# Grouped-query contexts computed already turned, from values held stationary and probabilities in high and low parts

## The reference, cut to what matters

```python
def gqa_attention(q, k, v):                 # q: 8 heads of 128, k and v: 2 heads of 128, 256 tokens
    ...
    def block(qblk):
        sc = jnp.einsum('bqkgd,bskd->bkgqs', qblk, k).astype(jnp.float32) * scale
        pr = jax.nn.softmax(sc, axis=-1).astype(v.dtype)
        return jnp.einsum('bkgqs,bskd->bqkgd', pr, v)
    ...
branch_b = gqa_attention(q, k, v) @ w_o_attn          # no causal mask here
mixed = jax.nn.sigmoid(gate_a) * branch_a + jax.nn.sigmoid(gate_b) * branch_b
```

## Time and profile before

| | |
|---|---|
| median of 3 runs | 1844.18 us (1843.59 to 1845.41) |
| the profiled execution | 1844.49 us, span 1842.7 us |
| TensorE matmul, busy | 1823.8 us, 99% of the span |
| VectorE, busy | 1186.5 us, 64% |
| ScalarE, busy | 983.3 us, 53% |
| GpSimd, busy | 127.6 us, 7% |
| DMA engines, mean busy share | 171 GB/s moved, 54.6% of 16 engines on the queue that loads weights |
| granted TensorE clock, mean | 0.999 of full speed |

### The profile page before, as it was taken

One profiled execution on the slowest core, in us unless ns is written; L12 is line 12 of the kernel. 1 busy time (PEld: TensorE's weight loads), 2 busy tenths in 40 slices (PEclk: granted clock), 3 DMA queues, 4 the chain that ended last, 5 costly groups with the idle time before them and its releaser, 6 DMA issues.

```text
span 1842.7 us, 24850 instructions
## 1 busy us (share of the span) xinstructions
PE 1823.8 (99%) x9042; PEld 1510.8 (82%) x9042; DVE 1186.5 (64%) x2022; ACT 983.3 (53%) x1571; POOL 127.6 (7%) x52
## 2 busy tenths in 40 slices
PE   8999999999999999999999999999999999999998
PEld 7887888888887888888878888888877788888886
DVE  6766873556766874455767667555677685675556
ACT  5546554444655654444645656544557366564444
POOL 0000018300000008500000000000000000000000
PEclk9999999999999999999999999999999999999999
DMA  7554665556555655556644445656556354556563
GB/s 243 157 139 137 194 194 173 186 190 197 167 143 142 195 173 182 171 183 185 219 126 143 143 149 172 204 161 209 173 173 195 109 163 132 166 173 187 177 210 111
DMA packets 167772, 315.33 MB, mean 171 GB/s; under 512 B 10250, under 2 KB 22748, under 8 KB 167524
## 3 DMA queue, kind: packets, MB, share of 16 engines
q1 hardware_dynamic: 167332, 313.14, 54.6%
q10 hardware_dynamic: 320, 0.60, 0.1%
HBM read 312.65 MB, written 1.05 MB: 170 GB/s over the span
## 4 chain that ended last, share of the span: by engine, by line
PE 98%; DVE 1%; DMA 0%; issue 0%; ACT 0%; ACTq 0%; DVEq 0%
PE acc L579 86%; PE mix L546 4%; PE mix L880 1%; PE mix L868 1%; PE mix L831 1%; PE mix L638 1%; PE mix L626 1%; PE mix L844 1%; PE mix L606 1%; PE mix L806 0%; PE mix L820 0%; PE mix L897 0%; PE mix L840 0%; PE mix L811 0%; PE mix L662 0%; PE mix L652 0%
## 5 line engine op out<-in xcount | busy, mean ns | idle before, releaser
L1081 ACT ACTIVATE hi<-raw 128x1024 fp32r<-128x1024 f32 (+2 forms) x600 | 616.6, 1032 | 523.0 <-PE acc L579 496.0
L1524 DVE TENSOR_TENSOR lo<-raw,hi 128x1024 fp32r<-128x1024 f32 (+3 forms) x552 | 647.3, 1188 | 243.3 <-ACT hi L1081 228.0
L579 PE MATMUL acc<-hi,xTh 128*128 128x512 f32 (+3 forms) x1760 | 690.1, 392 | 4.6 <-DVE lo L1524 1.4
L579 PE MATMUL acc<-hi,xTl 128*128 128x512 f32 (+3 forms) x1760 | 674.2, 383 | 0.0
L579 PE MATMUL acc<-lo,xTh 128*128 128x512 f32 (+3 forms) x1760 | 673.2, 382 | 0.0
L579 PEld LDWEIGHTS acc<-hi,xTh 128*128 128x128 f32 x1760 | 332.1, 189 | 75.9 <-issue 14.5
L579 PEld LDWEIGHTS acc<-hi,xTl 128*128 128x128 f32 x1760 | 331.7, 188 | 64.3
L579 PEld LDWEIGHTS acc<-lo,xTh 128*128 128x128 f32 x1760 | 332.4, 189 | 59.0 <-issue 1.0
L1052 POOL TENSOR_TENSOR lo<-raw,hi 128x1024 fp32r<-128x1024 f32 x48 | 127.4, 2681 | 635.7 <-ACT hi L1081 635.6
L579 PE MATMUL acc<-hi,hTh 128*128 128x512 f32 x432 | 169.2, 392 | 0.0
L579 PE MATMUL acc<-hi,hTl 128*128 128x512 f32 x432 | 168.4, 390 | 0.0
(11 more groups left out here) (232 smaller groups left out, 1516.7 us busy)
## 6 DMA issues: line engine op xcount, KB each, us to landing
raw<-in_w_in SPq DMA_DIRECT2D x192, 512.0 KB, 3.8
raw<-in_w_ffn_in SPq DMA_DIRECT2D x80, 512.0 KB, 4.4
raw<-in_w_mlp_up SPq DMA_DIRECT2D x64, 512.0 KB, 3.8
raw<-in_w_mlp_down SPq DMA_DIRECT2D x64, 512.0 KB, 4.5
raw<-in_w_ffn_out SPq DMA_DIRECT2D x44, 512.0 KB, 4.4
raw<-in_w_out SPq DMA_DIRECT2D x32, 512.0 KB, 4.1
raw<-in_w_o_gla SPq DMA_DIRECT2D x16, 512.0 KB, 3.7
raw<-in_w_o_attn SPq DMA_DIRECT2D x16, 512.0 KB, 3.7
```

Source lines behind the costliest of these rows:

```text
L579: last = nc.tensor.matmul(out, a[:, t * P:(t + 1) * P], w[:, slot, part, 0:c.n], start=(k == 0 and a is ah and w is L.hi), stop=(k == c.k_ ...
L1081: nc.scalar.activation(L.plan.part(L.hi, u), L.plan.part(L.raw, u), ACT.Copy).then_inc(*n.up("hi_ready"))
L1524: v.tensor_tensor(lo, raw, hi.bitcast(F32), ALU.subtract).then_inc(*n.up("low_by_dve"))
```

## The change

Values become the stationary operand and probabilities the moving one, so that a context comes out as features by tokens, which is what the output product wants. Both are split into high and low float32r parts, and a context is three products for each of the two key tiles, six matmuls of 256 columns (`gqa_context`). The probabilities are divided by their sums before they are turned (`probs_scaled`, VectorE), since the sums now belong to the moving columns. Of the turned probabilities ScalarE writes the high part (`probs_high`) and VectorE the low part (`probs_low`); the bank counts as drained after the low part. The contexts of a pair of heads are split the same way from bank 3 into `attnO` (`gqa_high`, `gqa_low`). The values are split once for each layer ahead of unit 48. The halves of turns ahead of the output product, their splits and the division of the contexts go away. On TensorE the context of head h-2 now stands after the first weight unit of iteration h, instead of before it. The table of semaphore counts changes with these, and `attnO` takes the place of gated-linear columns of `proj` that nobody reads any more.

The diff; left out are the table of counts, and the lines that hand the new tiles over. In `products` the key by which a unit of `branch_attn` waits for its stationary part also changes:

```diff
-            key = (c.ln, "lat", 1) if c.tag == "kv" else (c.ln, c.tag, "rows", t, j) if L.plan.by_rows(c, j) else (c.ln, c.tag, j)
+            key = (c.ln, "lat", 1) if c.tag == "kv" else (c.ln, "gqa", "o", j) if c.tag == "attn" else (c.ln, c.tag, "rows", t, j) if L.plan.by_rows(c, j) else (c.ln, c.tag, j)

```

```diff
@@ -443,7 +448,9 @@
         ks = at("ks", 0, [P, 2, NT, COLS], base=spare)
         soft = [at(f"soft{d}", 8 * d, [P, NT, COLS]) for d in range(2)]
         attn = at("attn", 16, [P, 2, NT, TOK])
-        attnT = at("attnT", 0, [P, 2, 4, P], base=spare)
+        attnT = [at(f"attnT{i}", 4 * n, [P, 2, NT, TOK], F32R, base=spare) for n, i in enumerate("hl")]
+        values = [at("valuesh", 20, [P, NT, AKV_H * A_D], F32R), at("valuesl", 10, [P, NT, AKV_H * A_D], F32R, base=spare)]
+        attnO = [at("attnOh", 0, [P, AQ_H, TOK], F32R, base=big), at("attnOl", 0, [P, AQ_H, TOK], F32R, base=big + IN2_COLS * 4)]
         pe_rows = at("pe_rows", 8, [P, NT, PLE], base=spare)
         embed = at("embed", 0, [P, NT, D], base=big + FFN // P * TOK * 4)
         ple_gate = at("ple_gate", 0, [P, NT, D], base=big)
...
@@ -469,7 +476,9 @@
                 return [a[:, k, :] for a in mobaT]
             if tag == "ret":
                 return [a[:, k, :] for a in retT]
-            at_k = {"lat": k, "kv": 2, "mla": k, "pe": k, "gla": k, "attn": k - 4}[tag]
+            if tag == "attn":
+                return [a[:, k, :] for a in attnO]
+            at_k = {"lat": k, "kv": 2, "mla": k, "pe": k, "gla": k}[tag]
             return [a[:, at_k, :] for a in oT]
 
         ident = cst("ident")
...
@@ -855,6 +865,23 @@
                 turn(("gqa", "q", j), lambda t, k: L.proj[:, t, at2(AQ) + k * P:at2(AQ) + (k + 1) * P], (2 * j, 2 * j + 1), among=among)
         turn_queries(0)
         turn(("gqa", "k", 0), lambda t, k: L.proj[:, t, at2(AK) + k * P:at2(AK) + (k + 1) * P], (0, 1))
+
+        def gqa_context(h):
+            g, i, kv = h // 2, h % 2, h // (AQ_H // AKV_H)
+            b, use = L.banks.get((ln, "gqa", "o", g), (3,))
+            if h == 0:
+                pe.wait_ge(*n.next("values_split"))
+            emptied(("gqa", "t", h))
+            if i == 0 and use:
+                pe.wait_ge(*n.at(f"bank{b}_drained", use))
+            vh, vl = (a[:, :, kv * A_D:(kv + 1) * A_D] for a in L.values)
+            ph, pl = (a[:, h % 2] for a in L.attnT)
+            for kt in range(NT):
+                for a, w in ((vh, ph), (vh, pl), (vl, ph)):
+                    last = nc.tensor.matmul(L.mix[:, b, i * TOK:(i + 1) * TOK], a[:, kt, :], w[:, kt, :],
+                                            start=(kt == 0 and a is vh and w is ph), stop=(kt == NT - 1 and a is vl))
+            if i == 1:
+                last.then_inc(*n.up(f"bank{b}_filled"))
         s.to(48)
         for j in range(2):
             emptied(("gqa", "q", j))
...
@@ -869,22 +896,10 @@
                                                                  L.kT[:, kv, :], **f32) for t in range(NT)], (0, 1, 2))
             if h >= AQ_H:
                 s.on(1)
-            if h >= 2:
-                g, i, kv = (h - 2) // 2, h % 2, (h - 2) // (AQ_H // AKV_H)
-                b, use = L.banks.get((ln, "gqa", "o", g), (3,))
-                emptied(("gqa", "t", h - 2))
-                if i == 0 and use:
-                    pe.wait_ge(*n.at(f"bank{b}_drained", use))
-                for t in range(NT):
-                    for kt in range(NT):
-                        last = nc.tensor.matmul(L.mix[:, b, (2 * t + i) * P:(2 * t + i + 1) * P], L.attnT[:, h % 2, 2 * t + kt, :],
-                                                L.proj[:, kt, at2(AV) + kv * P:at2(AV) + (kv + 1) * P], start=(kt == 0), stop=(kt == NT - 1))
-                if i == 1:
-                    last.then_inc(*n.up(f"bank{b}_filled"))
-            if h == 8:
-                pe.wait_ge(*n.next("rows_ready", NT))
-                turn_half("attn", 0, y_tile, (0, 1, 2))
+                gqa_context(h - 2)
             s.on(1 if 1 <= h <= AQ_H else 0)
+            if 2 <= h < AQ_H:
+                gqa_context(h - 2)
             if h == 1:
                 pe.wait_ge(*n.next("rows_ready"))
                 turn_queries(1, (0, 1, 2))
...
@@ -893,12 +908,9 @@
                 turn_half("gla", h // 3, y_tile, (0, 1, 2))
             s.on(1 if 1 <= h < AQ_H else 0)
             if 1 <= h <= AQ_H:
-                emptied(("gqa", "s", h - 1))
-                fill(("gqa", "t", h - 1), lambda b: [nc.tensor.transpose(L.mix[:, b, (2 * t + kt) * P:(2 * t + kt + 1) * P],
-                     L.attn[:, (h - 1) % 2, t, kt * P:(kt + 1) * P], L.ident) for t in range(NT) for kt in range(NT)], (0, 1, 2))
-        s.to(66)
-        pe.wait_ge(*n.next("rows_ready", NT))
-        turn_half("attn", 1, y_tile)
+                pe.wait_ge(*n.next("probs_ready"))
+                fill(("gqa", "t", h - 1), lambda b: [nc.tensor.transpose(L.mix[:, b, (2 * kt + t) * P:(2 * kt + t + 1) * P],
+                     L.attn[:, (h - 1) % 2, t, kt * P:(kt + 1) * P], L.ident) for kt in range(NT) for t in range(NT)], (0, 1, 2))
         merged = lambda t, k: L.proj[:, t, at2(G_A) + k * P:at2(G_A) + (k + 1) * P]
         s.to(71)
         pe.wait_ge(*n.next("rows_ready"))
...
@@ -1375,6 +1387,17 @@
         s.to(46)
         for j in range(2):
             empty(("gqa", "q", j), L.qT[:, 2 * j:2 * j + 2, :], 2 * TOK)
+        s.to(47)
+        nc.scalar.activation(L.values[0][:, :, :], L.proj[:, :, at2(AV):at2(AV) + AKV_H * A_D], ACT.Copy).then_inc(*n.up("values_high"))
+
+        def probs_high(h):
+            b = filled(("gqa", "t", h))
+            nc.scalar.activation(L.attnT[0][:, h % 2, :, :], L.mix[:, b, :], ACT.Copy).then_inc(*n.up("probs_high"))
+
+        def gqa_high(g):
+            b = filled(("gqa", "o", g))
+            nc.scalar.activation(L.attnO[0][:, 2 * g:2 * g + 2, :], L.mix[:, b, :], ACT.Copy).then_inc(*n.up("contexts_high"))
+
         s.to(48)
         for h in range(AQ_H + 2):
             if h < AQ_H:
...
@@ -1388,8 +1411,8 @@
                 last.then_inc(*n.up(f"bank{b}_drained"))
             if h >= AQ_H:
                 s.on(1)
-            if h == 8:
-                split_half("attn", 0)
+            if h >= 4 and h % 2 == 0:
+                gqa_high(h // 2 - 2)
             if h == AQ_H - 1:
                 s.on(1)
                 sigmoids(at2(G_A))
...
@@ -1399,14 +1422,14 @@
                 if h == 1:
                     for j in (2, 3):
                         empty(("gqa", "q", j), L.qT[:, 2 * j:2 * j + 2, :], 2 * TOK)
-                    empty(("gqa", "t", 0), L.attnT[:, 0, :, :], COLS)
+                    probs_high(0)
                 if h in (2, 5):
                     split_half("gla", h // 3, gla_gain(ln))
                 s.on(1 if 1 <= h < AQ_H else 0)
             if 2 <= h <= AQ_H:
-                empty(("gqa", "t", h - 1), L.attnT[:, (h - 1) % 2, :, :], COLS)
+                probs_high(h - 1)
+        gqa_high(3)
         s.to(66)
-        split_half("attn", 1)
         s.to(67)
         sigmoids(at2(G_B))
         s.to(71)
...
@@ -2141,6 +2164,30 @@
         tell("rows_ready")
         tell("params_free")
         tell("tmp_free")
+        dve.wait_ge(*n.next("values_high"))
+        link(v.tensor_tensor(L.values[1][:, :, :], proj[:, :, at2(AV):at2(AV) + AKV_H * A_D], L.values[0][:, :, :].bitcast(F32), ALU.subtract), "values_split")
+
+        def probs_low(h):
+            b, use = L.banks.get((ln, "gqa", "t", h))
+            dve.wait_ge(*n.next("probs_high"))
+            v.tensor_tensor(L.attnT[1][:, h % 2, :, :], mix[:, b, :].rearrange("p (k q) -> p k q", k=NT), L.attnT[0][:, h % 2, :, :].bitcast(F32), ALU.subtract)\
+                .then_inc(*n.up(f"bank{b}_drained"))
+
+        def gqa_low(g):
+            b, use = L.banks.get((ln, "gqa", "o", g))
+            dve.wait_ge(*n.next("contexts_high"))
+            v.tensor_tensor(L.attnO[1][:, 2 * g:2 * g + 2, :], mix[:, b, :].rearrange("p (h q) -> p h q", h=2), L.attnO[0][:, 2 * g:2 * g + 2, :].bitcast(F32), ALU.subtract)\
+                .then_inc(*n.up(f"bank{b}_drained"))
+
+        def probs_scaled(h):
+            b, use = L.banks.get((ln, "gqa", "s", h))
+            dve.wait_ge(*n.at(f"bank{b}_drained", use + 1))
+            at, sums = INVERSE + 2 * (h % 2), SUMS + 4 * (h // 2) + h % 2
+            link(v.reciprocal(col(at, 2), small[:, sums:sums + 3:2]))
+            for t in range(NT):
+                last = v.tensor_scalar(L.attn[:, h % 2, t, :], L.attn[:, h % 2, t, :], col(at + t), None, ALU.mult)
+            last.then_inc(*n.up("probs_ready"))
+
         s.to(48)
         for h in range(AQ_H + 2):
             if h < AQ_H:
...
@@ -2151,18 +2198,12 @@
                     .then_inc(*n.up("shift_ready"))
             if h >= AQ_H:
                 s.on(1)
-            if h >= 3 and h % 2 == 1:
-                g = (h - 3) // 2
-                key = ("gqa", "o", g)
-                b = filled(key)
```

(48 more changed lines are left out.)

## The result

The changed kernel takes **1849.19 us** (median of 9 executions, 1848.68 to 1850.39). The kernel before takes 1844.27 beside it (9 executions). The ratio is 1.0025, with a 95% interval of 1.0017 to 1.0033: slower by 4.9 us, or 0.25%. The prediction took 0.2% as the bound between same and slower, and that lies inside the interval, so the change is slower, but only just by that bound. The profiled execution took 1849.97 us, with a span of 1847.8.

The account below looks back on a forecast made before the run. TensorE's own queue was taken as the bound (98% of the chain); per layer -3.64 + 1.60 + 1.60 + 2.0 = +1.56, two layers +3.1, so 1847.3 us on the median, range 1840.5 to 1850.5.

Parts of the forecast that it names:

- likeliest case: Whole kernel: own saving less waits at heads 4, 6 and 8 gives 1847.3 us, range 1845.5 to 1849.1; chance 58%.
- TensorE's own saving, 7.3 us: Grouped-query stage: cheaper contexts and 16 fewer turns cut TensorE's work by 3.64 us a layer, 7.3 in all.
- The waits at heads 4 and 6, 1.60 us each: Contexts in iterations 4 and 6: exponentials, pair's high part, pair's low part, probabilities' low part delay TensorE 1.60 us each.
- The wait at head 8, 2.0 us: Context in iteration 8: late ScalarE copy and VectorE's branch product delay the low parts, costing TensorE 2.0 us.
- No wait at other heads: Contexts at odd heads and head 2: low part ready before the covering weight unit ends, odd heads with 1.1 us to spare.
- The low values are made before head 0: Start of the stage: the values' low part costs 0.7 us on VectorE and nothing on TensorE.
- as they are: Weight units, output product included: price taken as unchanged, 2.77 us for 12 matmuls, 5.46 for two.
- all waits hidden: Rival, contexts in the stage: no waits remain, the full 7.3 us gain stands, 1836.9 us; chance 10%.
- VectorE late: Slower rival, contexts 0 and 1, then odd heads: VectorE reaches scores over 1.1 us late, about 2.7 more, 1850.0; 17%.
- The contexts aren't cheaper: Rival, context matmuls: weights from changed tiles expose 0.08 us each, 7.7 on top, 1855 us; chance 5%.
- Only the late wait at h = 8: Rival, stage: only iteration 8's wait remains, -7.3 + 4.0, 1840.9 us; chance 10%.
- a clock that falls in the waits is none: TensorE's waits: dismissed as a rival, since after 1.19 us idle at 1345.83 matmuls still ran at 2.4 GHz.

Follow-up runs that it names:

- best: Changed kernel with pair outputs split in odd iterations, probabilities' low part before VectorE's unit in iterations 8 and 9, values' low part later, low contexts 512-byte aligned: 1837.09 us.
- swap_low: Changed kernel with, on VectorE in iterations 4, 6 and 8, the probabilities' low part ahead of the pair's low part: 1848.57 us, ratio 1.0023.
- ctx_before: Changed kernel with the context of head h-2 back ahead of the first weight unit in iterations 2 to 7: 1878.74 us, one execution.
- values_late: Changed kernel with the values' low part made in iteration 1, behind the scaling of head 0, instead of ahead of unit 48: 1849.08 us, ratio 1.0025.
- pair_odd: Changed kernel with each pair's output split in the odd iteration completing it, and iteration 8's probabilities' low part ahead of VectorE's unit: 1841.58 us, ratio 0.9983.
- high_first: Changed kernel with, on ScalarE in iterations 4 and 6, the pair's high part ahead of the new head's exponentials: 1843.47 us, ratio 0.9996.
- offset_256: Changed kernel with the turned contexts' low part 128 bytes further on, 256 off a multiple of 512: 1850.10 us, one execution.
- offset_64: Changed kernel with both parts of the turned contexts 64 bytes off a multiple of 512: 1851.31 us, one execution.

## Why the prediction was right, and where it was short

The range (1840.5 to 1850.5) holds 1849.19; the likeliest case's own range ended at 1849.1. The forecast 1847.3 was 1.9 us low, and the time fell just beyond the bound of 0.2% on which the chances for "same" and "slower" turned (46 and 40%). The direction and the waits were foreseen; that the time still lies in the range is owed to the room that the rivals gave it, as the costs that no step had, 2.4 us, all went one way.

- **TensorE's own saving, 7.3 us**: right. It can be seen bare in best, 7.31 us in the stages. A context of six takes 0.71 against the 0.72 of the sum. The Trainium skill (TensorE: Matmul & The Clock Gate, Back-to-back issue gap) gives about 81 ns for a sustained matmul of 128 columns. The trace doesn't agree: 0.89 us for eight such float32 matmuls is 111 ns each. That is nearly what a float32r matmul of twice the columns takes, 118 ns in a context of six without a wait, and from this the contexts' share of the gain comes.
- **The waits at heads 4 and 6, 1.60 us each**: right in place and in the chain of four pieces, a little long. The context ends 4.99 us after the scores (1040.32 to 1045.31); without a wait it would end 2.77 + 0.71 = 3.48 after them: 1.5. ScalarE's high part ends at 1042.97, +2.65 as forecast; but VectorE takes it up 0.03 later, not 0.10, and that is most of the difference. Why the pair's low part holds the context was told only by half. By the prediction it delays the probabilities' low part behind it; swap_low shows that the context waits for the pair's low part itself, which frees bank 3. "The new bank waits are on parts that a context waited for already" is wrong there, and it cost nothing only because in the order as written the probabilities' low part comes last.
- **The wait at head 8, 2.0 us**: right; the scores of head 7 end at 1066.84, and the context 12.09 us later, against 12.12 by the forecast's numbers, 10.11 of which are TensorE's own work.
- **No wait at other heads**: right for the contexts. ctx_before shows what the cover is worth: 1.83 us at each odd head comes to light when the unit is taken away, against 2.77 of cover.
- **Where it failed first**: "The low values are made before head 0, cost 0.7 on VectorE and nothing on TensorE, as the first context has room." I asked who waits for the low values, not what is queued behind them on VectorE: the first maximum, head 0's exponentials, and through the bank of head 0's scores the second turn of queries. The cost in the chain is 0.4 us in the first layer and 0.7 in the second; values_late gives back 1.3 in the stages. One of the prediction's own signs of being wrong, idle time at a unit whose weights are late, shows once: 0.17 us at 1504.72, ahead of the second stage.
- **Where it failed second**: the units of the output product were taken "as they are". Their stationary operand moved to another address, at 0.055 us a unit, 0.9 us in all. No step of mine looked at where the new tiles lie.
- **Outside the span**: 0.35 us that no step had.

So 3.1 became 2.7 by the shorter waits, plus 1.1 to 1.3, plus 0.9, plus 0.35: 5.1 to 5.3, against 4.9 between the medians and 5.5 between the profiled executions.

Of the rivals, "all waits hidden" is what the kernel does once the order is mended, the low values moved and the address put right (1836.9 forecast for it, 1837.1 measured in best). The order alone, pair_odd, gives 1841.6. "VectorE late" did not come about for the contexts; a relative of it, the turn of queries, did. "The contexts aren't cheaper" falls, at 0.71 us a context. "Only the late wait at h = 8" is what high_first makes of the kernel, not what the changed kernel does.

And one sentence was right for this kernel but on bad evidence: "a clock that falls in the waits is none". In the stages of the changed kernel the granted clock stays at 1.00. But the very stretch of the earlier trace rows that I gave as proof shows the clock falling in other executions, see below.

## What to carry to other kernels

When a single copy becomes a chain of two engines, follow each new instruction in both directions: who waits for its result, and what stands behind it in its queue. Here one 0.60 us copy that stood behind the exponentials instead of ahead of them cost 5.7 us, nearly twice the net loss that was forecast, and a subtraction whose result nobody needed soon cost 1.1 more in the stages. A helper engine needn't be full for this: VectorE was busy for 60 of the 88 us of the stage after the change. And a tile that is loaded as stationary operand should start where the others do: compare the distance of matmul starts by tile before taking "unchanged" products at their old price.

## What the runs showed of the hardware

**The address of a stationary tile counts.** One of two stationary parts, used by four of a unit's 12 matmuls, 128 bytes off a multiple of 256 makes a unit 2.775 us instead of 2.72; both parts 64 bytes off make it 2.80. Other offsets weren't tried. Here is the changed kernel, first matmuls of two consecutive units, 2.78 apart:

```profile
1085.45 0.40 PE L589 MATMUL acc<-hi,attnOh 128*128 128x512 f32 x1
...
1088.23 0.39 PE L589 MATMUL acc<-hi,attnOh 128*128 128x512 f32 x1
```

**The clock can fall after several short waits.** Where the two layers of the second block meet, TensorE idles four times within some 9 us (1.19, 0.73, 1.14 and 0.69 us). In 5 of 13 profiles (best, high_first, offset_256, offset_64, swap_low) the clock then fell for about 3.5 us; in the other eight, both of the kernel before among them, it stayed up with the same idle times. This is high_first, the same place as the earlier trace rows, with the matmuls 0.43 us apart from the fifth to the twelfth behind the last idle time:

```profile
1352.11 0.47 PE L589 MATMUL acc<-hi,xTh 128*128 128x512 f32 x1 [0.69 <-DVE lo L1549]
...
1353.68 0.63 PE L589 MATMUL acc<-hi,xTl 128*128 128x512 f32 x1
1354.11 0.63 PE L589 MATMUL acc<-hi,xTh 128*128 128x512 f32 x1
```

The granted clock of that stretch:

```profile
1352.00:1357.00 5.00, 4.89 (x15) 3.92 (x16) 3.13 (x7) 1.93 (x7) 0.00 (x0) 0.66 0.36 105
```

Eight matmuls at 0.43 instead of 0.23 are 1.6 us. Between the stages those profiles have 406.4 to 407.1 us and the others 404.8 to 405.6. That it comes and goes for one and the same kernel is likely but not shown, as each has one profile, the kernel before two: in values_late the three executions with a mean granted clock of 0.999 took 1847.2 to 1848.0 us and the five with 0.998 took 1848.9 to 1849.8. Such a fall is as large as the scatter of the executions, so effects of a microsecond are better read from landmarks in the stage than from medians. The waits of 1.26 to 1.83 us of idle in the stage, 16 us or more apart, never brought it about in the seven profiles that have them; a single wait of 4.02 or 4.03 did, all four times.
